# A mixture-of-experts decoder step: last splits behind the item branch, and a final stage with another order and TensorE adding gated rows

## The reference

```python
hf = h2                                     # (1056, 1024)
top_val, top_idx = top_k(hf @ w_router + b_router, 4)      # of 32 experts
probs = softmax(top_val)
gate = minimum(gu[:, :1024], 7); up = clip(gu[:, 1024:], -7, 7)   # gu = xs @ w_gu + b_gu
act = gate * sigmoid(1.702 * gate) * (up + 1)
out = (act @ w_down + b_down[expert]) * probs               # summed over a token's four experts
y = rmsnorm(x1 + g2 * moe, final_norm)
```

## Time and profile before

| | us |
|---|---|
| median of 3 runs | 2195.52 |
| the runs | 2192.89, 2195.52, 2197.51 |
| span of the profiled execution | 2192.6 |
| until the first item | 665.9 |
| the item loop | 1476.5 |
| after the loop | 50.2 |

### The profile page before, as it was taken

One profiled execution on the slowest core, in us unless ns is written; L12 is line 12 of the kernel. 1 busy time (PEld: TensorE's weight loads), 2 busy tenths in 40 slices (PEclk: granted clock), 3 DMA queues, 4 the chain that ended last, 5 costly groups with the idle time before them and its releaser, 6 DMA issues.

```text
span 2192.6 us, 38702 instructions
## 1 busy us (share of the span) xinstructions
PE 2059.1 (94%) x11946; PEld 1503.0 (69%) x11947; DVE 1621.2 (74%) x2213; ACT 1279.9 (58%) x1717; POOL 784.6 (36%) x997
## 2 busy tenths in 40 slices
PE   6998999999958999999999999999999999999995
PEld 4996766666647676676666677767676676777552
DVE  4533456666668687787777689988897798899667
ACT  3632443334316676676765568767776676877544
POOL 3224345555623233223331323433232233334124
PEclk7999999999969999999999999999999999999997
DMA  9767511211268787898887789999898898999665
GB/s 343 232 222 267 170 49 51 68 49 54 87 229 330 264 316 281 293 351 289 278 310 255 260 294 375 364 341 331 290 370 324 287 339 333 345 359 390 243 226 180
DMA packets 154530, 572.25 MB, mean 261 GB/s; under 512 B 22560, under 2 KB 41773, under 8 KB 120165
## 3 DMA queue, kind: packets, MB, share of 16 engines
q1 hardware_dynamic: 127405, 511.87, 62.1%
q0 software_dynamic: 25520, 56.53, 10.6%
q10 hardware_dynamic: 1552, 3.13, 0.4%
HBM read 521.36 MB, written 50.29 MB: 261 GB/s over the span
## 4 chain that ended last, share of the span: by engine, by line
PE 53%; DVE 6%; issue 6%; ACT 4%; DVEq 1%; DMA 0%; ACTq 0%; POOLq 0%
PE pg L2235 9%; PE pg L2236 9%; PE pg L2238 9%; PE py L2194 6%; PE py L2170 4%; PE py L2171 4%; PE py L2174 4%; PE pg L2208 3%; DVE lo L2459 3%; ACT hi L2371 2%; PE pt L2165 1%; PE pg L2228 1%; DVE pair L2477 1%; DVE pair L2473 1%; ACT sigm L2379 1%
## 5 line engine op out<-in xcount | busy, mean ns | idle before, releaser
L2235 PE MATMUL pg<-hi,xs 128*128 128x512 f32 x1056 | 429.4, 407 | 0.0
L2236 PE MATMUL pg<-lo,xs 128*128 128x512 f32 x1056 | 411.8, 390 | 0.0
L2459 DVE TENSOR_TENSOR lo<-spare,hi 128x1024 fp32r<-128x1024 f32 x264 | 306.3, 1221 | 85.2 <-ACT hi L2371 82.2
L2459 DVE TENSOR_TENSOR lo<-w_out,hi 128x1024 fp32r<-128x1024 f32 x272 | 312.4, 1220 | 59.2 <-ACT hi L2371 59.1
L2238 PE MATMUL pg<-hi,xs 128*128 128x512 f32 x1056 | 325.5, 389 | 0.0
L2459 DVE TENSOR_TENSOR lo<-raw,hi 128x1024 fp32r<-128x1024 f32 x264 | 314.1, 1220 | 7.1
L2371 ACT ACTIVATE hi<-spare 128x1024 fp32r<-128x1024 f32 x264 | 260.2, 1050 | 43.7 <-PE pg L2238 43.7
L2371 ACT ACTIVATE hi<-raw 128x1024 fp32r<-128x1024 f32 x264 | 271.0, 1053 | 25.1 <-PE pg L2238 24.2
L2371 ACT ACTIVATE hi<-w_out 128x1024 fp32r<-128x1024 f32 x272 | 265.5, 1050 | 32.4 <-SPq L2002 28.0
L2235 PEld LDWEIGHTS pg<-hi,xs 128*128 128x128 f32 x1056 | 198.3, 188 | 72.7 <-DVE lo L2459 13.3
L2170 PE MATMUL py<-hi,aT 128*128 128x512 f32 x528 | 218.8, 414 | 12.1 <-ACT aT L2383 5.5
(11 more groups left out here) (487 smaller groups left out, 3646.2 us busy)
## 6 DMA issues: line engine op xcount, KB each, us to landing
w_out<-in_w_gu SPq DMA_DIRECT2D x136, 1024.0 KB, 6.9
spare<-in_w_gu SPq DMA_DIRECT2D x132, 1024.0 KB, 10.3
raw<-in_w_down SPq DMA_DIRECT2D x132, 1024.0 KB
ada_w<-in_w_ada SPq DMA_DIRECT2D x4, 2048.0 KB
spare<-in_w_ada SPq DMA_DIRECT2D x4, 2048.0 KB
moe_rows<-small SPq DMA_DIRECT2D x9, 512.0 KB, 6.7
w_v<-in_w_in SPq DMA_DIRECT2D x2, 2048.0 KB, 17.4
w_i<-in_w_in SPq DMA_DIRECT2D x2, 2048.0 KB, 18.6
```

What stands on the lines that cost most here:

```text
L2235: pe.matmul(pg[u][b][:, :], xs[:, kt, 0, :], wh[:, u, :], start=False, stop=False)
L2236: pe.matmul(pg[u][b][:, :], xs[:, kt, 0, :], wl[:, u, :], start=False, stop=False)
L2459: dve.tensor_tensor(lo[q % RING][:, :, :], grain(q % GRAINS), hi[q % RING][:, :, :].bitcast(F32), ALU.subtract).then_inc(s["lo"], 1)
```

## The change

Three things are done together. ScalarE's splits 6 and 7 and VectorE's splits 5 to 7 of the next item move from the end of an item to the `head` of the next, behind the branch; the last item no longer makes them. `pT` and `bd` move from the ring buffers to `aT`, so they no longer wait for the loops' ends. And the final stage gets another order: the sample first, then tiles 0 to 7 (`order`, `place`). Tiles 0, 2, 4 and 6 (`PAIRED`) are no longer summed by VectorE: TensorE adds their gated `acc` rows into the PSUM banks through the identity (`add_rows`), ScalarE squares the banks in two halves and joins the two sums with an `Identity` and the root, and VectorE scales from the banks.

```diff
@@ in experts @@
-        pT = [hi[0][0:STACK, 0, :], hi[0][0:STACK, 1, :], sb("pTs", [E, NS])]
-        bd = hi[1]
+        stack = aT[0:STACK, :, :, :].rearrange("p k u t -> p (k u t)")
+        pT = [stack[:, 0:512], stack[:, 512:1024], sb("pTs", [E, NS])]
+        bd = stack[:, 1024:2048].rearrange("p (c n) -> p c n", c=2)
...
-        z = [py, pg[0], pg[1], pt]
+        z = [py, pt, pg[0], pg[1]]
...
+        order = [tiles[TILES]] + tiles[:TILES]
+        place = {t: p for p, (t, _) in enumerate(order)}
+        PAIRED = (0, 2, 4, 6)
@@ sync @@
-            for t, T in tiles:
-                if t == FIRST:
+            for t, T in order:
+                if t == TILES:
                     sp.wait_ge(s["act_end"], 1)
                     sp.wait_ge(s["dve_end"], 1)
                 sp.dma_start(acc[t][0:T, :], scratch["acc"][t * P:t * P + T, :]).then_inc(s[f"acc{t}"], 16)
-            for t, T in tiles:
-                sp.wait_ge(s["res"], t + 1)
+            for p, (t, T) in enumerate(order):
+                sp.wait_ge(s["res"], p + 1)
...
@@ tensor @@
-            for t, T in tiles:
+            for t, T in order:
                 for g in range(1 if t == TILES else 3):
...
+            def slot(t):
+                p = place[t]
+                if p == 0:
+                    pe.wait_ge(s["act_end"], 1)
+                elif p == 1:
+                    pe.wait_ge(s["dve_end"], 1)
+                elif p < 4:
+                    pe.wait_ge(s["pT"], p)
+                    pe.wait_ge(s["pT_lo"], p - 1)
+                elif p == 4:
+                    pe.wait_ge(s["biased"], 1)
+                elif order[p - 4][0] in PAIRED:
+                    pe.wait_ge(s["res"], p - 3)
+                else:
+                    pe.wait_ge(s["sum"], sum(1 for k in range(1, p - 3) if order[k][0] not in PAIRED))
+                return z[p % 4]
...
+            def add_rows(t, T):
+                pe.wait_ge(s["gated"], t + 1)
+                for c in range(2):
+                    last = pe.matmul(z[place[t] % 4][c][0:T, :], identm[0:T, 0:T], acc[t][0:T, c * 512:(c + 1) * 512], start=False, stop=True)
+                last.then_inc(s["paired"], 1)
 
-            residual_rows(*tiles[0])
-            for t in range(1, TILES):
+            bias_sample(*tiles[TILES])
+            for t in range(3):
                 residual_rows(*tiles[t])
-                bias_rows(*tiles[t - 1])
-            bias_rows(*tiles[TILES - 1])
-            pe.wait_ge(s["sum"], TILES - 3)
-            bias_rows(*tiles[TILES])
+            for t in range(3):
+                bias_rows(*tiles[t])
+            for t in range(3, TILES):
+                residual_rows(*tiles[t])
+                bias_rows(*tiles[t])
+                if t - 3 in PAIRED:
+                    add_rows(*tiles[t - 3])
+            for t in range(TILES - 3, TILES):
+                if t in PAIRED:
+                    add_rows(*tiles[t])
@@ scalar @@
                 act.activation(y[:, 0:512], py[0][:, :], ACT.Copy).then_inc(s["y0"], 1)
-                act.wait_ge(s["y_mm1"], i + 1)
+                wait_used(act, i, GRAINS - 2)
+                wait_used(act, i, GRAINS - 1)
                 act.activation(y[:, 512:1024], py[1][:, :], ACT.Copy).then_inc(s["y1"], 1)
+
+            def head(i):
                 for q in range(RING - 2, RING):
-                    split_hi(i, GRAINS + q)
+                    split_hi(i, q)
...
-            per_class(act, item)
+            per_class(act, item, head)
...
+            for p, (t, T) in enumerate(order):
+                if t in PAIRED:
+                    act.wait_ge(s["paired"], PAIRED.index(t) + 1)
+                    for c in range(2):
+                        act.activation(sq[0:T, c * 512:(c + 1) * 512], z[p % 4][c][0:T, :], ACT.Square, accum_out=ss[0:T, t, c:c + 1]).then_inc(s["ss_half"], 1)
+                    act.wait_ge(s["ss_half"], 2 * PAIRED.index(t) + 2)
+                    act.activation(ss[0:T, t, 0:1], ss[0:T, t, 0:1], ACT.Identity, scale=1.0 / D, bias=eps[0:T, :]).then_inc(s["ss"], 1)
+                    act.wait_ge(s["ss"], p + 1)
+                    act.activation(r[0:T, t:t + 1], ss[0:T, t, 1:2], ACT.Sqrt, scale=1.0 / D, bias=ss[0:T, t, 0:1]).then_inc(s["root"], 1)
...
@@ vector @@
             def head(i):
-                for q in range(RING, GU + 3):
+                for q in range(5, GU + 3):
                     split_lo(i, q)
...
-                for q in range(RING):
+                for q in range(5):
                     split_lo(i, GRAINS + q)
...
+                if t in PAIRED:
+                    for c in range(2):
+                        cut = slice(c * 512, (c + 1) * 512)
+                        last = dve.scalar_tensor_tensor(out=res[p % 3][0:T, cut], in0=z[p % 4][c][0:T, :], scalar=r[0:T, t:t + 1], in1=fnorm[0:T, cut],
+                                                        op0=ALU.mult, op1=ALU.mult)
...
-            for t in range(2):
-                gated(*tiles[t])
-            for t in range(2, ALL):
-                if t < TILES:
-                    gated(*tiles[t])
-                else:
-                    gated_sample(*tiles[t])
-                normed(*tiles[t - 2])
-            for t in range(ALL - 2, ALL):
+            summed_sample(*tiles[TILES])
+            normed(*tiles[TILES])
+            for t in range(1, TILES, 2):
+                summed(*tiles[t])
+                normed(*tiles[t - 1])
                 normed(*tiles[t])
```

More of the change, by code:

```diff
@@ L2329, in residual_rows @@
             def residual_rows(t, T):
+                banks = slot(t)
                 pe.wait_ge(s[f"x1{t}"], 16)
[L2331 to L2339, removed]
                 for c in range(2):
-                    pe.matmul(z[t % 4][c][0:T, :], identm[0:T, 0:T], x1[t][0:T, c * 512:(c + 1) * 512], start=True, stop=False)
+                    pe.matmul(banks[c][0:T, :], identm[0:T, 0:T], x1[t][0:T, c * 512:(c + 1) * 512], start=True, stop=False)
@@ L2355, in bias_rows @@
-                last.then_inc(s["bias"], 1)
-            residual_rows(*tiles[0])
-            for t in range(1, TILES):
-                residual_rows(*tiles[t])
-                bias_rows(*tiles[t - 1])
-            bias_rows(*tiles[TILES - 1])
-            pe.wait_ge(s["sum"], TILES - 3)
-            bias_rows(*tiles[TILES])
+                pe.wait_ge(s["bd_hi"], 1)
+                pe.wait_ge(s["bd_lo"], 1)
+                pe.wait_ge(s["pT_lo"], t // 4 + 1)
+                for c in range(2):
+                    last = pe.matmul(z[place[t] % 4][c][0:T, :], pT[t // 4][:, t % 4 * P:(t % 4 + 1) * P], bd[:, c, :], start=False, stop=t not in PAIRED)
@@ new lines, in bias_rows, with bias_sample @@
+                if t not in PAIRED:
+                    last.then_inc(s["bias"], 1)
+            def bias_sample(t, T):
+                banks = slot(t)
+                pe.wait_ge(s["pT"], 1)
+                pe.wait_ge(s["bdown"], 48)
+                for c in range(2):
+                    last = pe.matmul(banks[c][0:T, :], pT[2][:, :], bdown[0:E, c * 512:(c + 1) * 512], start=True, stop=True)
+                last.then_inc(s["bias_s"], 1)
+            def add_rows(t, T):
[3 more added lines that the diff above has]
+                last.then_inc(s["paired"], 1)
@@ L2434, in _ @@
                 rows_hi(0, half, pt[1 - half])
-            for q in range(5, RING):
-                split_hi(0, q)
+            split_hi(0, 5)
             act.wait_ge(s["table"], 16)
-            per_class(act, item)
+            per_class(act, item, head)
             act.activation(spark[:, 1:2], spark[:, 0:1], ACT.Sqrt).then_inc(s["act_end"], 1)
-            act.wait_ge(s["dve_end"], 1)
-            for j in range(3):
-                act.wait_ge(s["pT_ps"], j + 1)
+            for k, j in enumerate((2, 0, 1)):
+                act.wait_ge(s["pT_ps"], k + 1)
                 n, rows = (4 * P, STACK) if j < 2 else (NS, E)
@@ L2554, in _ @@
                 rows_lo(0, half, pt[1 - half])
-            for q in range(5, RING):
-                split_lo(0, q)
             dve.wait_ge(s["table"], 16)
@@ L2574, in _, with summed @@
             dve.tensor_tensor(second, bdown_g[E:2 * E, :].rearrange("p (c n) -> p c n", c=2), second.bitcast(F32), ALU.subtract).then_inc(s["bd_lo"], 1)
-            def gated(t, T):
-                dve.wait_ge(s["bias"], t + 1)
+            def summed(t, T):
+                dve.wait_ge(s["bias"], t // 2 + 1)
                 dve.wait_ge(s["gated"], t + 1)
```

50 lines of the change are left out of this document (22 added, 28 removed).

## The result

The changed kernel takes 2216.44 us (median of 4 runs, 2215.48 to 2217.54), before 2194.2 (4 runs, 2192.3 to 2197.51): a ratio of 1.0106, 95% interval 1.0094 to 1.0118. It is 22 us slower, where +2.5 was forecast and 2202.5 was the top of the range. The profiled execution took 2216.87 us, its span 2215.3.

A forecast was written before the change was run, and what follows sets the result against it. The prediction took TensorE to bound the loop, and a loop through four engines the changed final stage. Loop -2.2 plus stage +4.7 gave +2.5 us, span 2195.1; adding 2.9 to reach the median gave 2198.0 us, range 2192.0 to 2202.5.

The forecast's parts named there:

- Part 1: Expert loop, splits moved behind the branch: no work added for an item that runs, -2.2 us (bounds -3.3 and -0.1).
- split 6 comes 0.2 to 0.3 us later: ScalarE in eight items without a rest that follow another such: lateness inside the free slack, taken as 0.2 us in all.
- The free 0.35 us: VectorE's ninth split: about 0.35 us of lateness past 5.95 us costs nothing, each further microsecond costs one.
- Rival (D): Loop: ScalarE's branch shows in eight items; 1.0 us late costs 0.65 each, 5.2 in all, 2203 us; chance 0.15.
- the item at 1983.64: Loop item at a group boundary: ScalarE's split 6 comes 1.2 us later, 0.85 beyond what is free, +0.9 us.
- the -3.3: Three group-boundary items following an item with a rest: VectorE's ninth split starts 1.1 us sooner each (bounds -2.0 and -3.3).
- Part 2: Stage after the loop: +0.5 for the rounds' end, +0.6 last store, +3.6 clock, +4.7 us (bounds +1.1 and +7.3).
- TensorE ... has its part of this ready by 2160 at full clock: Final stage: TensorE, starting at about 2147.5, is ready before `normed(0)`, which ends at 2164.6.
- The rounds: Final stage: a loop through four engines, 10.1 us a round, two rounds; two clock restarts of 1.8 us come on top.
- (B): Final stage: the clock doesn't fall in the rounds; -1.1 us in sum, 2194.4 us; chance 0.12.
- (C): Final stage: the rounds hide and GpSimd sets the pace; stage -6.8, -9.0 with the loop, 2186.5 us; chance 0.10.
- (E): Final stage: ScalarE's new `Identity` brings table loads of 1.28 us, two per paired tile; +7.7, 2205.7 us; chance 0.04.

The follow-up runs named there:

- spark_once: The changed kernel with the one-element sigmoid once ahead of the loop and none in it: 2232.02 us, ratio 1.0176.
- spark_first: The changed kernel with each item's one-element sigmoid put ahead of ScalarE's two moved splits: 2200.30 us, ratio 1.0026.
- vector_move: The kernel before with only VectorE's three splits moved behind its branch, ScalarE's left in place: 2188.81 us, ratio 0.9973.
- stage_busy4: stage_alone with four TensorE products of zeros added ahead of the residual rows of tiles 4 and 6: 2197.76 us, ratio 1.0022.
- stage_early: stage_alone with TensorE adding the gated rows of tiles 2, 4 and 6 earlier: 2189.62 us, ratio 0.9977.
- no_load_before: The kernel before with the sigmoid once ahead of the loop and none in it: 2234.69 us, ratio 1.0180.
- loop_pause: Changed loop, sigmoid once ahead of it, one unneeded ScalarE Copy in items without a rest, and the final stage of before: 2181.99 us, ratio 0.9947.
- stage_alone: The kernel before, its loop kept, with only the changed final stage: 2200.27 us, ratio 1.0034.

## Why the prediction was wrong

**The step that failed** is the first sentence of Part 1, "No work is added for an item that runs", and with it ScalarE's "split 6 comes 0.2 to 0.3 us later". A table load of 1.28 us was added to each of the 33 items. It was priced in the earlier trace rows, where it stands ahead of the first function behind the branch, and I read it as the sigmoid's alone. My reading of the reason is that behind the loop's branch the table loaded before is not known when the program is compiled, so one is loaded for whatever function comes first; here that became a Copy, and the table taken for it was not the sigmoid's, which needed its own. The traces show where the loads stand, not how they were placed, but spark_once fits this reading: with the same table on all ways into the loop, it has no load at all, though a Copy is the first function behind the branch there too. The Trainium skill has the rule that this rests on in "ScalarE activation tables: per-element evaluation and per-set limits", section "Table sets in the compiler and the runtime": loads are placed block by block. The runs agree in part: where the known table does for both blocks (spark_first, spark_once) no load is put into the second.

**The arithmetic around it held.** The free 0.35 us and one for one beyond it gave 1.06 for a delay of 1.41; the item grew 1.04. Rival (D) had the effect, a late split 6, but not its cause, and at a lateness of 1.0 in eight items only; the second kind, with nothing free, grew by 1.4, and the three boundary ones lost their gain. The loop came to +19.1 between the marks, where -2.2 was forecast. The forecast's own term for the item at 1983.64, +0.9, was right once the load was gone (0.84 in spark_first); the same run shows 0.3 us in the items of the second kind for which the forecast had nothing.

**The boundaries:** the -3.3 was right to a tenth (vector_move). In the changed kernel the load ate it.

**Part 2** was right in its mechanism: +6.5 us where +4.7 was forecast, inside its bounds. Counted from the start of the last scatter, the sample's first addition came 8.7 us later (8.8 forecast) and `normed(0)` 21.8 us (19.5). The missing 2.3 are the one mis-sized term there: "TensorE ... has its part of this ready by 2160 at full clock". Its clock was at the lower level from 2163.59 on (0.50, and 0.53 from 2167.1 to 2170.6, then 1.00), 3.6 us for four pieces, a third restart that I had not counted. The sample's last addition took 3.18 us, not 2.1, but lies beside TensorE's work. The rounds took 11.66 and 11.46, where 10.1 and 1.8 for the clock make 11.9, and that both terms are real is shown by the rows of stage_busy4. The end lay 3.5 us behind the last operation, not 3.1.

**The rivals.** (B) falls: the clock did fall, and keeping it up took 4 us off the stage in the profile, though the medians don't part the two kernels. (C) came close for another kernel: with the rounds cut to 5.6 us (stage_early) the stage is 45.0, 4.0 below before, where (C) had 6.8. (E) falls: no table load stands before the Identity, as "ScalarE: Activation LUTs" of the Trainium skill, section "Table sets: the hidden batching unit", has it. The list lacked a rival in which the compiler adds an instruction; I had looked for what the diff adds.

**Adding to the median:** I put 2.9 us on the span; in the changed kernel's profiled execution the time lies 1.6 above its span. This hid a part of the error: the span was forecast at 2195.1 and came to 2215.3, 20.2 us more, while the forecast of 2198.0 and the median lie 18.4 apart. And the lower end of the range, 2192.0, doesn't follow from the terms named for it: -3.3 and +1.1 on the median give 2193.3.

What stays open: what holds the scatter up, how short a pause VectorE may make for it, and why the moment of the issue goes with its length. Of the fourteen long ones in spark_once and no_load_before ten ended 1.5 us behind the start of a pause of under 0.1 us, and four behind the end of a split with none.

## What to carry to other kernels

When an activation is moved across a branch, ask which function is now the first behind it: that one may pay for a table load (1.28 us, 33 times). A stall that looks wasted can be what lets another engine in; before it is removed, look at what runs only while it lasts, here GpSimd's scatter. Where several engines pass a bank round in turn, issue the next tile's work ahead of the instruction that waits for this one.

## What the runs showed that I had not expected

- A scatter issued by GpSimd beside an unbroken train of VectorE subtractions with two inputs in SBUF, about 0.59 us ahead of a split's end, occupies GpSimd for 12.4 to 13.5 us, with a pause of 0.67 us in the train 4.4, with 0.45 at that end 2.15. VectorE itself waited 6.68 us for the landing of a long one. Issued 0.26 us ahead of a split's end, it takes 1.7 us beside the same unbroken train.
- A kernel whose loop loads no table at all is 40 us slower than before (no_load_before); with one Copy of about 1 us in its place and the splits moved (loop_pause) it is 12.7 us faster.
- Of two operations of 32x1024 with both inputs in SBUF, the multiplication, which began 0.12 us before GpSimd's first product (2170.00), took 1.21 us, and the addition, which began in the midst of that product, 3.18. In stage_alone the multiplication, too, began in the midst of GpSimd's first product (at 2155.91, the product at 2154.70) and took 2.21.
